# First pair of expert places in strict turns of wide and narrow quarters, with a shorter early load

## The chip, the cores and the metric

The kernel runs on one core of a Trainium2 chip. The metric is the device time of one execution in microseconds, as the median of several runs. TensorE multiplies matrices, VectorE and ScalarE do elementwise work, GpSimd a few powers, and SyncE (SP) issues nearly all DMAs.

## The reference

A hybrid decoder trunk of two layers on 256 tokens of width 1024, float32. Each layer has a mixer (four mLSTM heads beside a diagonal state-space block, joined by an output projection) and a channel mixer. In layer 0 that is a dense SwiGLU of width 2816. In layer 1, which this case is about, it is a routed SwiGLU of eight experts of width 3584, of which each token uses two:

```python
logits = (xt @ w_router).astype(jnp.float32) + b_router.astype(jnp.float32)
top_v, top_i = lax.top_k(logits, TOP_K)
gates = jax.nn.softmax(top_v, axis=-1)
combine = jnp.einsum('tk,tke->te', gates, jax.nn.one_hot(top_i, N_EXPERTS, dtype=jnp.float32))
out = jnp.zeros_like(xt)
for e in range(N_EXPERTS):
    out = out + combine[:, e:e + 1].astype(xt.dtype) * swiglu(xt, w_gate[e], w_up[e], w_down[e])
```

A final RMSNorm follows. The kernel computes an expert only for the tokens that chose it.

## The kernel before

After the router come eight *places*, worked off in pairs (0, 1), (2, 3), (4, 5), (6, 7). Their shapes are fixed by ITEMS = "AEBECDDD" (line 72): A holds 128 tokens, E 32, B 128 + 32, C 64 + 32, D 64. A text below calls the quarters of the first place A0 to A3, those of the second E0 to E3, and the first quarter of the third place B0. Which expert goes to which place is decided on the chip by how many tokens chose it, except that the first place always holds expert 0. Tokens beyond the places' room would be worked off in a loop behind them (MORE, `n_over`), whose length is read from the data.

Each place is cut into four *quarters* of 896 columns of the expert's width. A quarter is: gate and up products (`gate_up`; lines 2279 for 128 tokens, 2293 for 64, 2308 for 32), SiLU on ScalarE and the product on VectorE (`hidden`), the transposes of that (line 2343), and the down products (`down`; lines 2370 and 2381), accumulated in PSUM over the four quarters. The down products of a quarter are issued after the gate and up products of the next one. Between them, at fixed positions of the pair (`between`), stand the gathers of the next place's tokens (line 2256), the transposes of the pick matrix (line 2396) and the scatter of the last pair's result (line 2409). TURNS says in which order the quarters of the two lanes of a pair follow each other: lane 0 is the first place of the pair. FIRST_DONE is the position at which ScalarE copies the first place's finished result out of PSUM.

The weights pass through a ring in SBUF of MSLOT = 18 slots. A gate or up unit (two of eight row blocks, 896 KB) takes one slot and a down unit (1792 KB) two, so a quarter takes 12. `place_units` deals the slots out in the order in which the units were listed, that is in TensorE's order with a quarter's down units behind the gate and up units of the next quarter, and notes for each unit the event that releases the slots it overwrites. A unit of A's gate or up is released when its own matmuls are done, since A has no 32-token part; B's are released only when the whole gate-and-up work of the quarter, with its narrow part (line 2308), is done. SP issues the units in that order and waits before each for its release (`load_unit`, DMA lines 893 and 896). SP has one queue, so a unit that waits holds up all behind it.

The ring lies over the trunk's own weight ring and work space. The *early* units are those with nothing before them in their slots; SP issues them when the trunk's last layer has read the chunks there (`wait_unused`, `hm_ready`), all with expert 0, before it waits on `ranks_ready`, the event that VectorE gives when the list of experts (`n_list`, line 1801) stands. Behind it, SP reads each place's expert number with `value_load` at the first unit of the place.

VectorE writes the list in two parts: `first_tiles` (the order of the experts) right after A's tokens are taken, and `second_tiles` (the overflow) at position 2 of pair 0.

Of the kernel before, what the change touches and what calls it, by code (L numbers as in the profile page):

```python
# [60 lines left out]
MC = 4  # L61
# [11 lines left out]
NI = len(ITEMS)  # L73
# [2 lines left out]
MORE = 6  # L76
COLS = NI + MORE
TMAX = max(CAPS)
TURNS = [(0, 0, 1, 0, 1, 0, 1, 1)] + [(0, 1) * MC] * (NI // 2 - 1)
FIRST_DONE = [len(a) - a[::-1].index(0) for a in TURNS]  # L80


class Experts:


    def __init__(self, last):
# [9 lines left out]
        for p in range(NI // 2):  # L96
            done = [0, 0]
            for pos, lane in enumerate(TURNS[p]):
                self.steps.append((p, pos, 2 * p + lane, done[lane]))
# [368 lines left out]
def trunk_kernel(nc, x, norm_mix, w_in, conv_qk, b_igate, b_fgate, norm_mlstm, s5_a_re, s5_a_im, s5_log_dt,  # L468
# [4 lines left out]
    experts = Experts(banks.last)  # L473
# [4 lines left out]
    with ctx:  # L478
# [236 lines left out]
        def wait_drained(eng, name):  # L715

            _, who, n, _ = banks.at[name]
            eng.wait_ge(drained[who], n)
# [51 lines left out]
        def m_wait_drained(eng, key, k=None):  # L770

            _, who, n, _, _ = experts.at[key]
            eng.wait_ge(m_drained[who], later(n, experts.per_who[who], k))
# [13 lines left out]
        def unit(it, c, kind, h):  # L787

            s, size, _, _ = experts.slot[(it, c, kind, h)]
            return m_ring[:, s:s + size, :].rearrange("p s n -> p (s n)")  # L790
# [23 lines left out]
        def _(sp):  # L814
# [81 lines left out]
                    sp.dma_start(v3(unit(it, c, kind, h), UK),  # L896
                                 src.rearrange("e (k p) n -> p (e k) n", p=P)).then_inc(full, 16)

            early = [u for u in experts.units[:experts.base[3]] if not experts.slot[u[:4]][3]]
            for u in early:  # L900
                s, size, _, _ = experts.slot[u[:4]]
                assert u[0] == 0
# [1582 lines left out]
```

## Time and profile before

| | us |
|---|---|
| median of 3 runs | 1463.04 |
| lowest, highest | 1456.69, 1465.71 |
| the profiled execution, its own time | 1457.26 |
| its span | 1455.1 |
| TensorE matmul busy | 1341.7 (92%) |
| VectorE busy | 470.8 (32%) |
| ScalarE busy | 278.4 (19%) |
| DMA, read | 421.2 MB, 290 GB/s over the span |

The span is the time from the first to the last instruction of the profiled execution. TensorE's busy time is modelled and overlaps its weight loads. The mean granted clock of TensorE was 0.979 of full speed. Times of views are counted from the start of the span. The expert stage begins at 558.8 us, with the first wide matmul of A0, and fills the rest.

### The profile page before, as it was taken

The numbers are of one execution on the slowest core, as the hardware profiler recorded it, in microseconds if no ns is written. First come the engines' busy times: TensorE is split into PE (matmuls) and PEld (weight loads), VectorE is DVE, ScalarE is ACT, GpSimd is POOL, SyncE is SP. The second block draws the span as 40 slices with busy tenths as digits, with TensorE's granted clock in tenths as the row PEclk, the third lists the DMA queues.
The fourth block names the chain that finished last, engine by engine and source line by source line (L and its number), as shares of the span: only waits on it lengthen the run. The fifth ranks groups of instructions, "written<-read, shape, count | busy, mean of one in ns | idle before, by whom it ended". The sixth has DMA issues, their size and how long they took to land.

```text
span 1455.1 us, 18657 instructions
## 1 busy us (share of the span) xinstructions
PE 1341.7 (92%) x7760; PEld 758.9 (52%) x7760; DVE 470.8 (32%) x1049; ACT 278.4 (19%) x515; POOL 98.5 (7%) x115
## 2 busy tenths in 40 slices
PE   6988899999799878999999999999999999987775
PEld 5845489999685535544455444444433344332322
DVE  7995965555589533041010100100110100000002
ACT  2541344443254100000011010001101101000001
POOL 4530000000442000000000000000000000000000
PEclk9999999999999989999999999999999999999999
DMA  9533345436221248799999959889999999999994
GB/s 286 153 116 116 115 164 185 174 116 244 75 87 59 101 191 332 250 363 414 413 411 416 411 213 410 338 353 401 410 411 416 410 410 416 410 412 415 410 414 199
DMA packets 126734, 423.50 MB, mean 291 GB/s; under 512 B 21632, under 2 KB 23864, under 8 KB 118456
## 3 DMA queue, kind: packets, MB, share of 16 engines
q1 hardware_dynamic: 121464, 421.75, 74.2%
q10 hardware_dynamic: 5184, 0.52, 0.4%
q8 instruction: 64, 1.05, 0.3%
q14 instruction: 22, 0.18, 0.0%
HBM read 421.20 MB, written 1.05 MB: 290 GB/s over the span
## 4 chain that ended last, share of the span: by engine, by line
PE 74%; DMA 14%; DVE 8%; issue 1%; SPq 1%; ACT 1%; POOL 0%; DVEq 0%; ACTq 0%
PE psall L2279 13%; DMA m_ring<-in_moe_w_down_dram 12%; PE psall L2370 11%; PE psall L2293 8%; PE psall L2308 6%; PE psall L1992 4%; PE psall L2381 3%; PE psall L2210 3%; PE psall L2090 3%; PE psall L2212 3%; PE psall L2211 3%; PE psall L2157 2%; PE psall L2256 2%; PE psall L2343 2%; PE psall L2409 2%; PE psall L2192 1%
## 5 line engine op out<-in xcount | busy, mean ns | idle before, releaser
L2293 PE MATMUL psall<-m_ring,xeT 128*64 128x448 f32 x1024 | 202.6, 543 | 22.5 <-DMA m_ring<-in_moe_w_up_dram 21.5
L2370 PE MATMUL psall<-m_ring,hidT 128*64 128x512 f32 (+1 forms) x672 | 201.0, 597 | 17.2 <-DMA m_ring<-in_moe_w_down_dram 16.4
L2279 PE MATMUL psall<-m_ring,xeT 128*128 128x448 f32 x512 | 195.7, 543 | 0.8 <-DVE xeT L1857 0.8
L2293 PEld LDWEIGHTS psall<-m_ring,xeT 128*64 128x64 f32 x1024 | 73.6, 137 | 139.9 <-issue 138.8
L2279 PEld LDWEIGHTS psall<-m_ring,xeT 128*128 128x128 f32 x512 | 97.3, 191 | 94.1 <-issue 92.9
L2370 PEld LDWEIGHTS psall<-m_ring,hidT 128*64 128x64 f32 (+1 forms) x672 | 72.6, 154 | 136.3 <-issue 120.1
L1879 DVE TENSOR_TENSOR hid<-e_silu,psall 64x448 f32<-64x448 f32 x32 | 19.9, 623 | 354.6 <-ACT e_silu L1231 352.5
L1577 DVE TENSOR_TENSOR w_lo<-ring,w_hi 128x1024 fp32r<-128x1024 f32 x66 | 80.5, 1225 | 68.0 <-ACT w_hi L1185 67.9
L2308 PE MATMUL psall<-m_ring,xeT 128*32 128x448 f32 x1024 | 102.0, 542 | 0.0
L2210 PE MATMUL psall<-hnT_hi,w_hi 128*128 128x256 f32 x352 | 99.6, 283 | 1.4 <-DVE hnT_lo L1715 1.4
L2212 PE MATMUL psall<-hnT_hi,w_lo 128*128 128x256 f32 x352 | 99.5, 283 | 0.0
L2211 PE MATMUL psall<-hnT_lo,w_hi 128*128 128x256 f32 x352 | 98.9, 281 | 0.0
L1992 PE MATMUL psall<-hnT,ring 128*128 128x256 f32 x384 | 87.1, 386 | 3.0 <-DMA ring<-in_w_in_dram 1.3
L961 POOL TENSOR_TENSOR small<-small,neg_half 128x1 f32<-128x1 f32 (+2 forms) x14 | 13.6, 974 | 1080.1 <-DVE small L1313 970.0
L1875 DVE TENSOR_TENSOR hid<-e_silu,psall 128x448 f32<-128x448 f32 x16 | 9.9, 622 | 227.0 <-PE psall L2279 226.0
L1185 ACT ACTIVATE w_hi<-ring 128x1024 fp32r<-128x1024 f32 x66 | 69.2, 1060 | 63.5 <-PE psall L2212 35.9
L1992 PEld LDWEIGHTS psall<-hnT,ring 128*128 128x128 f32 x384 | 73.3, 193 | 14.5 <-issue 2.1
L1245 ACT ACTIVATE hidT<-psall 128x224 f32<-128x224 f32 (+5 forms) x48 | 22.3, 481 | 266.9 <-PE psall L2343 266.7
L2210 PEld LDWEIGHTS psall<-hnT_hi,w_hi 128*128 128x128 f32 x352 | 66.7, 189 | 2.2 <-issue 1.4
L2211 PEld LDWEIGHTS psall<-hnT_lo,w_hi 128*128 128x128 f32 x352 | 66.6, 189 | 0.8
L2212 PEld LDWEIGHTS psall<-hnT_hi,w_lo 128*128 128x128 f32 x352 | 66.3, 188 | 0.0
L2308 PEld LDWEIGHTS psall<-m_ring,xeT 128*32 128x32 f32 x1024 | 30.4, 109 | 63.6 <-issue 63.0
(326 smaller groups left out, 1473.3 us busy)
## 6 DMA issues: line engine op xcount, KB each, us to landing
m_ring<-in_moe_w_gate_dram SPq DMA_DIRECT2D x128, 896.0 KB, 19.9
m_ring<-in_moe_w_up_dram SPq DMA_DIRECT2D x128, 896.0 KB, 17.1
m_ring<-in_moe_w_down_dram SPq DMA_DIRECT2D x64, 1792.0 KB, 19.1
ring<-in_w_in_dram SPq DMA_DIRECT2D x10, 2048.0 KB, 13.0
ring<-in_ffn_w_gate_dram SPq DMA_DIRECT2D x5, 2048.0 KB, 10.5
ring<-in_ffn_w_up_dram SPq DMA_DIRECT2D x5, 2048.0 KB, 7.7
ring<-in_ffn_w_down_dram SPq DMA_DIRECT2D x5, 2048.0 KB, 8.0
ring<-in_w_out_dram SPq DMA_DIRECT2D x4, 2048.0 KB, 7.9
```

Source lines behind the costliest of these rows:

```text
L1185: nc.scalar.activation(ffn_split(n, w_hi), ffn_raw(n), ACT.Copy).then_inc(ffn_hi, 1)
L1577: V.tensor_tensor(ffn_split(n, w_lo), ffn_raw(n), ffn_split(n, w_hi).bitcast(F32), ALU.subtract).then_inc(ffn_lo, 1)
L1992: ins = M(bank(name)[:, i * SEQ:(i + 1) * SEQ], w[:, k, a:a + P], hnT[:, k, :], start=(k == 0), stop=(k == KT - 1))
L2090: ins = M(bank(n)[:, :], hnT[:, k, n[2] * P:(n[2] + 1) * P], v3(chunk((n[0], l)), KT)[:, k, :], start=(k == 0), stop=(k == KT - 1))
L2210: M(y, hi[:, k, :], hnT_hi[:, k, :], start=(k == 0), stop=False)
L2211: M(y, hi[:, k, :], hnT_lo[:, k, :], start=False, stop=False)
L2212: ins = M(y, lo[:, k, :], hnT_hi[:, k, :], start=False, stop=(k == KT - 1))
L2279: ins = M(m_bank(key)[:, 0:MH], x[:, i, 0:P], weights(kind, i, s), start=(i == 0), stop=(i == KT - 1))
L2293: ins = M(m_bank(key)[64 * n:64 * n + 64, 0:MH], x[:, i, 0:64], weights(kind, i, s), start=(i == 0), stop=(i == KT - 1))
L2308: ins = M(m_bank(key)[q:q + 32, 0:MH], x[:, i, base:base + 32], weights(kind, i, s), start=(i == 0), stop=(i == KT - 1))
L2370: ins = M(y, hidT[:, r, 0:shape[0]], rows(r, 512 * n, 512), **ends)
L2381: ins = M(ps[7][32 * q:32 * q + 32, cols:cols + 256], hidT[:, r, base:base + 32], rows(r, 256 * q, 256), **ends)
```

## The change

The first pair takes the turns that the other pairs have. The early list ends at the first unit of another place than the first, or at the first unit whose slot is taken, whichever comes first.

```diff
-TURNS = [(0, 0, 1, 0, 1, 0, 1, 1)] + [(0, 1) * MC] * (NI // 2 - 1)
+TURNS = [(0, 1) * MC] * (NI // 2)
 FIRST_DONE = [len(a) - a[::-1].index(0) for a in TURNS]
...
-            early = [u for u in experts.units[:experts.base[3]] if not experts.slot[u[:4]][3]]
+            early = []
+            for u in experts.units[:experts.base[3]]:
+                if u[0] or experts.slot[u[:4]][3]:
+                    break
+                early.append(u)
             for u in early:
                 s, size, _, _ = experts.slot[u[:4]]
                 assert u[0] == 0
```

Before, pair 0 runs A0 A1 E0 A2 E1 A3 E2 E3, and the early units are the eight of A0, the eight of A1 and the first down unit of A0. After, it runs A0 E0 A1 E1 A2 E2 A3 E3. The ring's first 18 slots are then listed as A0's eight, E0's eight and A0's first down unit, and only the first eight are early.

## Rows read from the trace of the kernel before

**Rows 1.** The page's DMA issues: tile, queue, count, KB each, us to landing.
```profile
m_ring<-in_moe_w_gate_dram SPq DMA_DIRECT2D x128, 896.0 KB, 19.9
...
m_ring<-in_moe_w_down_dram SPq DMA_DIRECT2D x64, 1792.0 KB, 19.1
```

**Rows 2.** Windows: stretch, us; busy us (instructions) of each engine; clock, DMA share, GB/s.
```profile
640.00:750.00 110.00, 110.00 (x552) 54.82 (x553) 17.86 (x73) 9.13 (x18) 0.00 (x0) 1.00 1.02 413
...
840.00:861.00 21.00, 21.00 (x102) 9.44 (x104) 1.24 (x2) 1.09 (x2) 0.00 (x0) 1.00 0.28 111
...
1300.00:1400.00 100.00, 75.31 (x369) 29.00 (x365) 4.98 (x8) 5.92 (x11) 0.00 (x0) 1.00 1.02 413
```

**Rows 3.** Timeline of SP's queue around the list: start, duration, line, transfer, count.
```profile
533.52 9.26 SPq L896 DMA_DIRECT2D m_ring<-in_moe_w_up_dram  x4
542.83 2.20 SPq L893 DMA_DIRECT2D m_ring<-in_moe_w_down_dram  x1
...
565.13 0.33 SPq L893 DMA_DIRECT2D m_ring<-in_moe_w_down_dram  x1
```

**Rows 4.** Line 896 from 480 to 700 us: issue to landing.
```profile
DMA to landing us min/median/max: 4.7/10.1/22.8
```

**Rows 5.** Windows around the router and A's first two quarters.
```profile
535.00:558.00 23.00, 15.49 (x74) 11.17 (x72) 8.13 (x59) 3.54 (x7) 0.00 (x0) 0.69 1.03 412
565.00:585.00 20.00, 20.00 (x69) 11.08 (x67) 1.24 (x2) 1.09 (x2) 0.00 (x0) 1.00 0.95 327
...
585.00:590.00 5.00, 5.00 (x25) 3.65 (x25) 0.42 (x1) 1.09 (x2) 0.00 (x0) 0.70 0.40 159
```

**Rows 6.** Timeline of VectorE: the cast that writes the expert list.
```profile
562.90 0.17 DVE L1801 CAST n_list<-over 128x8 int32<-128x8 f32 x1
```

**Rows 7.** Timeline of SP's queue where a new place's first unit follows.
```profile
982.79 1.17 SPq L893 DMA_DIRECT2D m_ring<-in_moe_w_down_dram  x2
984.72 0.38 SPq L896 DMA_DIRECT2D m_ring<-in_moe_w_gate_dram  x1
```

**Rows 8.** Timeline of TensorE in pair 0: start, duration, line, operands, count [idle before].
```profile
558.77 24.32 PE L2279 MATMUL psall<-m_ring,xeT 128*128 128x448 f32 x64 [0.78 <-DVE xeT L1857]
582.92 3.65 PE L2256 MATMUL psall<-pick,hn 128*128 128x32 f32 x32
586.41 1.60 PE L2343 MATMUL psall<-ident,hid 128*128 128x128 f32 x7
587.81 25.50 PE L2279 MATMUL psall<-m_ring,xeT 128*128 128x448 f32 x64
613.14 12.18 PE L2370 MATMUL psall<-m_ring,hidT 128*128 128x512 f32 x28
...
626.10 6.22 PE L2308 MATMUL psall<-m_ring,xeT 128*32 128x448 f32 x64
...
644.37 0.60 PE L2396 MATMUL psall<-ident,pickg 128*128 128x128 f32 x4
...
670.12 3.23 PE L2381 MATMUL psall<-m_ring,hidT 128*32 128x256 f32 x56
673.28 1.13 PE L2343 MATMUL psall<-ident,hid 128*128 128x128 f32 x7
...
728.30 3.53 PE L2256 MATMUL psall<-pick,hn 128*128 128x160 f32 x24
...
743.68 1.25 PE L2256 MATMUL psall<-pick,hn 128*128 128x160 f32 x8
...
753.72 3.23 PE L2381 MATMUL psall<-m_ring,hidT 128*32 128x256 f32 x56 [1.66 <-DMA m_ring<-in_moe_w_down_dram]
756.88 1.04 PE L2343 MATMUL psall<-ident,hid 32*128 32x32 f32 x7
757.85 24.32 PE L2279 MATMUL psall<-m_ring,xeT 128*128 128x448 f32 x64
```

**Rows 9.** Window of the list's second part on VectorE (the third busy number).
```profile
634.00:651.00 17.00, 17.00 (x50) 8.51 (x49) 13.96 (x81) 0.95 (x2) 0.00 (x0) 1.00 1.02 417
```

## The prediction, made before the changed kernel was run

> **What bounds the kernel now.** I read the page's DMA issues first: one quarter of an expert is eight units of 896 KB (gate and up) and two of 1792 KB (down), so 12 ring slots of 896 KB, and 32 quarters are 384 slots [rows 1]. Then the stretches. While the expert stage runs freely the DMA share is 1.02 at 413 GB/s, with TensorE busy all the time: 896 KB is 0.9175 MB, so a slot costs 2.22 us and a quarter 26.7 us. At 840 to 861 the share is 0.28: there the stream stands, because the B place's units come free only after its narrow matmuls, and TensorE sets the pace. At 1300 to 1400 the stream is full again and TensorE has idle time; the chain of waits names the transfers there [rows 2]. So the stage has three parts: pair 0 (558.8 to 757.9), near balance; pair 1, led by TensorE; the rest, led by the stream, which restarts from where TensorE's last pair 1 quarter released slots. A shift of the start of B's first quarter (757.9) is therefore handed to the end in full, while a late stream alone has slack in pair 1: about 0.72 x 21 = 15 us at 840 to 861.
>
> **What the old order does with its head start.** SP issues the 17 early units (18 slots) by 545.0 and then has nothing to issue until 565.1, when the first slots of A's quarter 0 come free [rows 3]. The 20 us at 565 to 585 ran at 327 GB/s, and 585 to 590 at a share of 0.40 [rows 5]: with a full ring the stream waits for TensorE. That is where a head start is given back.
>
> **What the change does.** TURNS for pair 0 becomes A0 E0 A1 E1 A2 E2 A3 E3 (A is the wide place, E the narrow one). The unit list follows it, and so does the ring. The early list ends after A0's eight gate and up units; E0's eight and A0's down now wait for the expert list. No instruction of an engine is added or removed, no byte either; FIRST_DONE moves from 6 to 7, so that ScalarE's copy of A's result comes one position later, after the quarter that it needs.
>
> *Taken from the head start:* 10 slots x 2.22 = 22 us of transfers, which before were issued ahead of the list. They can't start before VectorE has cast the list, 562.90 + 0.17 [rows 6]. SP then reads the expert's number; between the last down unit before a new item and its first gate unit the queue shows 983.96 to 984.72, 0.8 us [rows 7]. So the first issue is at 564.0. SP waits there longer than before, but queued behind it are only these same loads; the load of the norm's gains stands ahead of the wait, as before.
>
> *When slots land.* Slots 9 to 18 are free at once. Later ones: slot n needs slot n-18 released. A1's last two (27, 28) need E0's first two, released by 590, with their turn at 606; E1's last two (39, 40) need A1's first two, 613 against 633; A1's down (44) needs A1's sixth unit, 626 against 642; E2's last (64) needs A1's down, 655 against 688. The release is at least 15 us ahead each time. So it runs unbroken at 2.22 us a slot. A unit took 4.7 us to land at the least [rows 4]. Slot n lands at 568.7 + 2.22 (n - 9): E0's last (16) 584.2, A0's down (18, 20) 588.7 and 593.1, E1's last (40) 637.5, A1's down (42, 44) 641.9 and 646.4, E2's last (64) 690.8, A2's down (66, 68) 695.2 and 699.7, E3's last (88) 744.1, A3's down (92) 753.0. In the old order slot 92 (E2's down) released TensorE at 753.7 [rows 8]. So both streams reach the end of pair 0 at the same moment: the old one had 22 us of lead and lost them while the ring was full.
>
> *TensorE's chain, new order* [rows 8]. A's gate and up 24.3, E's 6.15, A's down 12.2, E's down 3.2, A's transposes 1.1 (first time 1.4), E's 1.0, E's gather 3.5, B's 3.4 + 1.2, the pick's transposes 0.5 (these are mostly differences of neighbouring starts, as TensorE's records overlap). From 558.8: A0, gather, transposes 588.0; E0 594.1, A0's down 606.3, transposes 607.3; A1, E0's down, pick, transposes 636.4; E1, A1's down, transposes 655.8 (slots 42 and 44 just in time); A2, E1's down, transposes 684.4. **Now it waits:** E2's last units are wanted at 689.0 and land at 690.8 (1.8), A2's down wanted at 692.3 lands at 695.2 (2.9). Down and transposes end at 708.4; A3, gather, E2's down, transposes 741.7; E3 747.9; A3's down 760.1, transposes 761.1. B's first quarter starts at 761.1 instead of 757.9. The work is the same; waits are 4.7 us instead of 1.7 (752.06 to 753.72). That is +3.2 us.
>
> *Vector and Scalar.* The second part of the list (14 us of VectorE's work at 634 to 651 [rows 9]) now follows A1's product. It ends near 650; E1's product then waits for it and is wanted at 654.8 after A1's down. That down is the cover; without it the part would cost some 6 us. The final copies of A (position 7) lie beside B's 24 us. Both at nothing.
>
> *The clock.* A1's gate and up took 25.50 instead of 24.32, with a granted clock of 0.70 at 585 to 590 [rows 5, 8]: the lower level, 1.2 GHz, for a part of it, behind the short matmuls of gather and transposes. One more such fall is 0 to 1.2 us. In the stretch at 1300 to 1400 TensorE stands idle for short times many times over and the clock is 1.00 [rows 2]. I take 0.8, between the ends, since the two new waits are longer than those. [...]
>
> **Sum:** 3.2 + 0.8 = +4 us. Unknown costs: stream rate and landing -1.7 (no wait left at all, chain without the old 1.7) to +8 (slots landing 4 to 5 us later than the formula). Against the profiled execution: 1457.3 + 4 = 1461.3 (span 1455.1 + 4). That execution is 5.8 us under the median shown, 1463.0, and the runs spread from 1456.7 to 1465.7; in the median's terms 1467. I name 1466.5, a little toward the profile.
>
> **Rivals.**
> *R1, the head start is paid in full.* Place: E0 and after. If all that follows is led by the stream, 10 slots later is 22 us later: 1485. For it: the stream is full from 640 to 750 [rows 2]. Against it: in the old order it idles at 585 to 590 with a full ring [rows 5], and TensorE leads pair 1. It decides, beyond 1%, once slot 68 lands after 711 instead of 699.7, which is a mean of 380 GB/s over 60 slots; units fed one by one ran at 327 [rows 5], and 60 slots at that rate would take 168 us, 35 more than at 413. So it needs a stream that starves for slots. The Trainium skill (DMA: Bandwidth & Descriptors, Rules for kernel authors) says to issue a DMA early, compute, and wait for it late; taken alone it speaks against this change, and by it the price is those 22 us. Chance 0.12 (half of it in full, the rest 10 to 20 us).
> *R2, no wait is left.* The old order's own waits go, the stream lands 5 us earlier than my formula, and TensorE runs through pair 0: 558.8 + 197.4 = 756.2, -1.7 us: 1461. For it: the formula's landing time is one for a lone unit, and the waits are small. Against it: slot 92 of the old order lands within 1 us of the formula's time for the new one. It turns on whether slots 64 and 66 land by 689.0 and 690.6. Chance 0.12.
> *R3, faster.* The router's stretch gains from a quiet DMA: at 535 to 558 the share is 1.03 and the clock 0.69 [rows 5]. Yet TensorE waits there for VectorE's short steps, not for transfers. At most a few us, and over 1% only if something outside this account moves. Chance 0.04.
> *Forecast* (+2 to +8, no change that can be told): 0.72.
>
> **Numbers.** About 1% (14.6 us) is what a measurement of this kernel can tell from no change. Forecast and R2 lie inside it; of R1 some 0.10 lies beyond, of R3 0.03. Faster 0.03, same 0.87, slower 0.10. The range adds to the forecast's bounds (1461 to 1471 in the median's terms) the spread of the medians that the runs allow, some 4 us below and 6 above: 1457 to 1477; it leaves out R1 nearly whole, and R3's far end.
>
> **What would show it.** In the profile after: first E0 load at about 564 and a DMA share near 1.0 from 566 to 750; E0's narrow matmuls at 588 without a wait; waits of 2 to 5 us for transfers around 690 to 700; B's first wide matmul at 760 to 764; from there each line of TensorE shifted by the same 3 to 6 us, and a span near 1459. It is wrong if pair 0 shows holes in the stream (R1), if B starts at or before 757 (R2), or if pair 1 gives the shift back, which would mean that TensorE didn't lead it.

## The result, and the profile after

The changed kernel takes 1463.48 us (median of 20 runs, 1459.78 to 1467.82) against 1458.60 us for the kernel before in the same comparison. The ratio is 1.0031, 95% interval 1.0019 to 1.0042: 4.5 us, between 2.8 and 6.1 (the two medians differ by 4.9), so slower by less than a measurement of three runs could tell. The median of three runs shown ahead, 1463.04, was at the high end of the kernel before; 20 runs put it 4.4 us lower. The profiled execution has a span of 1458.9 us, 3.8 more than before.

Windows of the changed kernel: stretch, us; busy us of each engine; clock, DMA share, GB/s.

```profile
565.00:585.00 20.00, 20.00 (x67) 10.95 (x65) 1.24 (x2) 1.09 (x2) 0.00 (x0) 1.00 1.01 391
585.00:590.00 5.00, 5.00 (x36) 3.29 (x39) 0.42 (x1) 1.09 (x2) 0.00 (x0) 0.72 1.01 427
640.00:750.00 110.00, 106.17 (x532) 51.74 (x524) 17.29 (x71) 7.24 (x15) 0.00 (x0) 0.98 1.02 413
690.00:700.00 10.00, 6.50 (x31) 2.10 (x24) 1.24 (x2) 1.07 (x2) 0.00 (x0) 0.83 1.01 425
840.00:861.00 21.00, 21.00 (x69) 10.15 (x71) 1.24 (x2) 1.09 (x2) 0.00 (x0) 1.00 0.47 185
1300.00:1400.00 100.00, 76.63 (x378) 29.65 (x374) 3.74 (x6) 6.29 (x12) 0.00 (x0) 1.00 1.02 413
```

Read them against [rows 2, 5]. At 565 to 585 the stream moves 391 GB/s instead of 327, and at 585 to 590 it is full where it stood at a share of 0.40. It doesn't run out of free slots any more, because it starts behind. Its rate when full is the same 413 GB/s. TensorE now has 3.8 us of idle time at 640 to 750, where it had none. In pair 1 (840 to 861) there is still a hole, a smaller one: 0.47 instead of 0.28.

SP's queue around the expert list, and VectorE's cast that writes the list:

```profile
526.97 4.33 SPq L896 DMA_DIRECT2D m_ring<-in_moe_w_up_dram  x4
531.71 0.35 SPq L914 DMA_DIRECT2D bT<-in_norm_final_dram  x1
564.29 0.40 SPq L896 DMA_DIRECT2D m_ring<-in_moe_w_gate_dram  x1
...
570.59 3.00 SPq L893 DMA_DIRECT2D m_ring<-in_moe_w_down_dram  x2
```

```profile
563.14 0.17 DVE L1805 CAST n_list<-over 128x8 int32<-128x8 f32 x1
```

The queue is silent from 532.1 to 564.3. The first load stands 0.98 us behind the cast's end. All ten remaining slots of the first round are issued by 573.6.

TensorE in pair 0 and at the start of pair 1, down to E3's down products (the last row): start, duration, line, operands, count, [idle time before, what ended it].

```profile
559.01 24.32 PE L2283 MATMUL psall<-m_ring,xeT 128*128 128x448 f32 x64 [0.78 <-DVE xeT L1861]
...
588.19 7.42 PE L2312 MATMUL psall<-m_ring,xeT 128*32 128x448 f32 x64
...
608.72 24.32 PE L2283 MATMUL psall<-m_ring,xeT 128*128 128x448 f32 x64
...
638.04 6.22 PE L2312 MATMUL psall<-m_ring,xeT 128*32 128x448 f32 x64
...
657.38 24.32 PE L2283 MATMUL psall<-m_ring,xeT 128*128 128x448 f32 x64
...
685.85 4.72 PE L2312 MATMUL psall<-m_ring,xeT 128*32 128x448 f32 x48
692.94 3.16 PE L2312 MATMUL psall<-m_ring,xeT 128*32 128x448 f32 x16 [2.37 <-DMA m_ring<-in_moe_w_up_dram]
697.23 12.26 PE L2374 MATMUL psall<-m_ring,hidT 128*128 128x512 f32 x28 [1.13 <-DMA m_ring<-in_moe_w_down_dram]
...
743.56 6.22 PE L2312 MATMUL psall<-m_ring,xeT 128*32 128x448 f32 x64
750.52 12.25 PE L2374 MATMUL psall<-m_ring,hidT 128*128 128x512 f32 x28 [0.74 <-DMA m_ring<-in_moe_w_down_dram]
...
763.68 24.32 PE L2283 MATMUL psall<-m_ring,xeT 128*128 128x448 f32 x64
...
797.77 3.23 PE L2385 MATMUL psall<-m_ring,hidT 128*32 128x256 f32 x56
```

Three waits for transfers, at E2's last units, at A2's down and at A3's down, make 4.24 us; before there was one of 1.66 [rows 8]. E0's narrow matmuls took 7.42 us instead of 6.22 at a granted clock of 0.72 (585 to 590), which stands for the 1.2 us that A1 lost in the same place before. And the last 16 matmuls of E2, behind the 2.37 us wait, took 3.16 us; 16 of the same kind behind a 1.08 us wait in a run below took 1.71. B0 begins 204.7 us behind A0 instead of 199.1. The chain of waits between 670 and 780 goes through the last two of the three transfers:

```profile
678.35 18.75 DMA m_ring<-in_moe_w_down_dram
...
697.23 12.26 PE psall L2374 x28
...
730.82 19.56 DMA m_ring<-in_moe_w_down_dram
...
750.52 12.25 PE psall L2374 x28
```

So A2's down starts when slot 66 lands, A3's down when slot 90 lands, and what TensorE lost ahead of them only shortened its waits.

The chain that ended last names the same transfer as before, a down unit at the end of the last pair, 3.8 us later: it is followed from 1413.84 (before 1409.99) to TensorE's last down products at 1440.66 (before 1436.82).

```profile
1413.84 26.77 DMA m_ring<-in_moe_w_down_dram
1440.62 0.04 issue
1440.66 3.68 PE psall L2374 x16
```

### The profile page after: what moved, and what is told of

The parts are those of the page before. It is cut to its first block, busy times and chain, and to the rows that moved or that the text cites. A ratio compares the mean times of both kernels' runs of the same rounds, so it can differ in the third digit from the quotient of the medians.

```text
span 1458.9 us, 18655 instructions
## 1 busy us (share of the span) xinstructions
PE 1343.2 (92%) x7760; PEld 757.4 (52%) x7760; DVE 470.5 (32%) x1049; ACT 278.1 (19%) x515; POOL 98.0 (7%) x115
## 4 chain that ended last, share of the span: by engine, by line
PE 73%; DMA 15%; DVE 8%; issue 1%; ACT 1%; SPq 1%; POOL 0%; DVEq 0%; ACTq 0%
DMA m_ring<-in_moe_w_down_dram 13%; PE psall L2283 13%; PE psall L2374 12%; PE psall L2297 8%; PE psall L2312 5%; PE psall L1996 4%; PE psall L2214 3%; PE psall L2216 3%; PE psall L2094 3%; PE psall L2215 3%; PE psall L2385 3%; PE psall L2161 2%; PE psall L2260 2%; PE psall L2413 2%; PE psall L2347 2%; PE psall L2196 1%
## 5 line engine op out<-in xcount | busy, mean ns | idle before, releaser
L2374 PE MATMUL psall<-m_ring,hidT 128*64 128x512 f32 (+1 forms) x672 | 201.2, 597 | 19.4 <-DMA m_ring<-in_moe_w_down_dram 18.6
```

Source lines behind the costliest of these rows:

```text
L2374: ins = M(y, hidT[:, r, 0:shape[0]], rows(r, 512 * n, 512), **ends)
```

## The experiments

Theory 1: the change costs what the stream of weights lacks at E2 and at A's downs, because 10 slots are loaded behind the list instead of ahead of it; the strict turns cost nothing themselves. Theory 2: the turns cost it. R1: the lost head start is paid in full. Edits are shown against the changed kernel; those of old_late, old_pair1 and old_pair12 are made to the kernel before.

The beginning of A0 differs between profiled executions by up to 10 us, though nothing ahead of it differs but the loads. So the stage is compared from A0's start (computed from the timelines; the last column is the start of TensorE's last down products, which the last transfer releases).

| kernel | A0 | B0 - A0 | C0 - A0 | last down - A0 | ratio to before (95%) |
|---|---|---|---|---|---|
| before | 558.8 | 199.1 | 454.9 | 878.1 | |
| changed | 559.0 | 204.7 | 458.6 | 881.7 | 1.0031 (1.0019 to 1.0042) |
| strict_head17 | 559.6 | 198.7 | 454.5 | 877.8 | 1.0004 (0.9992 to 1.0017) |
| old_cut8 | 566.5 | 199.3 | 455.3 | 878.4 | 1.0000 (0.9988 to 1.0013) |
| strict_early9 | 556.8 | 200.5 | 454.7 | 878.0 | 1.0006 (0.9990 to 1.0022) |
| strict_late | 563.7 | 218.9 | 475.0 | 898.2 | 1.0125 (1.0105 to 1.0145) |
| old_late | 559.1 | 199.1 | 455.0 | 878.3 | 1.0006 (0.9989 to 1.0022) |
| old_pair1 | 564.7 | 199.4 | 454.6 | 868.4 | 0.9931 (0.9907 to 0.9955) |
| strict_pair1 | 559.4 | 204.9 | 459.5 | 873.2 | 0.9964 (0.9948 to 0.9979) |
| old_pair12 | 561.9 | 201.2 | 456.6 | 867.5 | 0.9906 (0.9887 to 0.9924) |

### strict_head17: the new turns with the whole head start

```diff
-                if u[0] or experts.slot[u[:4]][3]:
+                if experts.slot[u[:4]][3]:
                     break
...
-                load_unit(u, slice(0, 1))
+                load_unit(u, slice(u[0], u[0] + 1))
```

> Strict turns in pair 0 as in the changed kernel, but all 17 units with free slots are issued ahead of the list again: E0's gate and up are loaded with expert 1's weights instead of those that the list names, so this part of the result is another. Theory 1 (the late transfers cost it): slots 9 to 18 are there by 560, no wait near 690, B0 starts at 757 to 759, ratio to the kernel before 0.999 to 1.001, some 4 us under the changed kernel. Theory 2 (the order of the turns costs it, through later copies and narrower cover): B0 stays near 763, ratio 1.003.

This kernel leaves out the look-up of the expert for E0's gate and up and takes expert 1's, so its result is another, with the same bytes and the same matmuls.

Measured: 1.0004. TensorE of this kernel around 690:

```profile
686.41 6.22 PE L2311 MATMUL psall<-m_ring,xeT 128*32 128x448 f32 x64
692.56 12.28 PE L2373 MATMUL psall<-m_ring,hidT 128*128 128x512 f32 x28
...
758.26 24.32 PE L2282 MATMUL psall<-m_ring,xeT 128*128 128x448 f32 x64
```

E2 and A2's down follow each other without a wait and at full speed, and B0 comes 198.7 us after A0, 0.4 earlier than in the old order. The old order's 199.1 us contain a wait of 1.66 for a transfer and these 198.7 none, so TensorE's own chain is 1.3 us longer in the new turns, and the wait that they avoid pays for it. On balance the turns cost nothing that can be measured; Theory 2 falls.

### old_cut8: the old turns with only eight units ahead

```diff
-TURNS = [(0, 1) * MC] * (NI // 2)
+TURNS = [(0, 0, 1, 0, 1, 0, 1, 1)] + [(0, 1) * MC] * (NI // 2 - 1)
...
-                if u[0] or experts.slot[u[:4]][3]:
+                if len(early) == 8:
                     break
```

> The old turns, with only A0's eight units ahead of the list: A1's eight and A0's first down unit wait for it. Theory 1: slot n lands at 568.7 + 2.22 (n - 9); A1's last unit lands at 584 and is wanted behind 588, slot 92 lands at 753.0 against 753.7 before, so the cut of the head start alone costs +0.5 us (0 to +2.5), ratio 1.000 to 1.002. Rival R1 (the head start is paid in full): +22 us, 1.015. Theory 2: 1.000, as it blames the turns.

Measured: 1.0000. The same 22 us of transfers are moved behind the list, and nothing is lost. SP's queue, then TensorE:

```profile
570.84 2.32 SPq L896 DMA_DIRECT2D m_ring<-in_moe_w_gate_dram  x4
573.20 3.72 SPq L896 DMA_DIRECT2D m_ring<-in_moe_w_up_dram  x4
576.96 2.97 SPq L893 DMA_DIRECT2D m_ring<-in_moe_w_down_dram  x2
```

```profile
566.51 24.32 PE L2283 MATMUL psall<-m_ring,xeT 128*128 128x448 f32 x64 [0.78 <-DVE xeT L1861]
595.54 25.60 PE L2283 MATMUL psall<-m_ring,xeT 128*128 128x448 f32 x64
...
761.64 3.23 PE L2385 MATMUL psall<-m_ring,hidT 128*32 128x256 f32 x56 [1.75 <-DMA m_ring<-in_moe_w_down_dram]
```

The one wait is the old one, at E2's down: 1.75 us instead of 1.66. R1 falls: in this order the head start beyond eight units buys nothing. So neither half of the change costs anything alone that can be measured; the cost is that of both together. In the kernel before, slots 64 and 66 are A3's last unit and E1's down, wanted at 715 and 718 (A3 starts at 693.68 and reaches its last unit 21 us on):

```profile
693.68 24.32 PE L2279 MATMUL psall<-m_ring,xeT 128*128 128x448 f32 x64
717.93 3.23 PE L2381 MATMUL psall<-m_ring,hidT 128*32 128x256 f32 x56
...
792.05 4.75 PE L2381 MATMUL psall<-m_ring,hidT 128*32 128x256 f32 x56
```

In the strict turns they are E2's last unit and A2's down, wanted some 25 us sooner, at about 690 and 693, while a stream that starts at the list brings them at 693 and 697. (The last row, E3's down in the kernel before, is used further down.)

### strict_early9: one more unit ahead

```diff
-                if u[0] or experts.slot[u[:4]][3]:
-                    break
-                early.append(u)
+                if u[0] == 0 and not experts.slot[u[:4]][3]:
+                    early.append(u)
...
-            for u in experts.units[len(early):experts.base[3]]:
+            for u in [u for u in experts.units[:experts.base[3]] if u not in early]:
```

> Strict turns, and A0's first down unit (2 slots, expert 0, known ahead) is issued ahead of the list beside A0's eight, out of its place in the queue. Theory 1: every slot from 19 on lands 4.4 us earlier than in the changed kernel; the waits there of 2.37, 1.13 and 0.74 us shrink to under 1 in all, and the fall of the clock behind the first goes with them (1.6 us). Ratio to the kernel before 1.000 to 1.001, B0 at 758 to 760. Theory 2: ratio 1.003, B0 near 763.

Measured: 1.0006. Two slots, 4.4 us of transfers, take back 4.1 us at B0:

```profile
683.59 6.22 PE L2311 MATMUL psall<-m_ring,xeT 128*32 128x448 f32 x64
690.89 12.26 PE L2373 MATMUL psall<-m_ring,hidT 128*128 128x512 f32 x28 [1.08 <-DMA m_ring<-in_moe_w_down_dram]
...
744.15 12.26 PE L2373 MATMUL psall<-m_ring,hidT 128*128 128x512 f32 x28 [0.71 <-DMA m_ring<-in_moe_w_down_dram]
```

The 2.37 us wait is gone, and with it the slow matmuls behind it; the waits at the two downs stay, 1.79 us in all where I had expected under 1. This kernel has the changed one's turns and computes the same, without a cost that can be measured (its B0 still comes 1.5 us later than before, its C0 no longer).

### strict_late and old_late: the same late list in both orders

```diff
             sp.wait_ge(ranks_ready, 1)
+            sp.wait_ge(m_ready, experts.free[("uh", 0, 0, 1)])
```

> The changed kernel, but SP waits for the list and also for A0's sixth unit to be used (near 577 instead of 564). Theory 1: pair 0 is led by the stream from E0 on, all slots land 13 us later, and nothing gives it back: B0 near 776, +13 us over the changed kernel, ratio to the kernel before 1.011 to 1.013. If the stream had slack in pair 0 (R2's view, waits only by chance) the shift would be under 8 us, ratio under 1.009.

> The kernel before, but SP waits for the list and also for A0's sixth unit to be used (near 577 instead of 565), as strict_late does with the strict turns. Theory 1: 18 slots are already there, TensorE needs slot 20 at 618 and E0's at 626, and the stream's idle time between 585 and 625 takes up the 13 us: 0 to +2 us, ratio 1.000 to 1.001. So the same delay costs 13 us in the one order and head start and nothing in the other. If a late list costs the same in both, the ratio is 1.009.

Measured: 1.0125 and 1.0006. With the strict turns SP's first load comes 19.35 us behind A0's start instead of 5.28, so 14.1 later, and B0 comes 14.2 us later:

```profile
583.07 0.40 SPq L896 DMA_DIRECT2D m_ring<-in_moe_w_gate_dram  x1
```

```profile
599.60 1.71 PE L2313 MATMUL psall<-m_ring,xeT 128*32 128x448 f32 x16 [2.21 <-DMA m_ring<-in_moe_w_up_dram]
604.08 1.71 PE L2313 MATMUL psall<-m_ring,xeT 128*32 128x448 f32 x16 [2.77 <-DMA m_ring<-in_moe_w_up_dram]
608.38 13.95 PE L2375 MATMUL psall<-m_ring,hidT 128*128 128x512 f32 x28 [2.59 <-DMA m_ring<-in_moe_w_down_dram]
...
658.35 1.71 PE L2313 MATMUL psall<-m_ring,xeT 128*32 128x448 f32 x16 [1.08 <-DMA m_ring<-in_moe_w_up_dram]
```

E0 already waits, which it does not in the changed kernel. Over the runs the delay costs 0.0094, 13.7 us, as expected; this one execution ends 16.5 us later than the changed one, and of the 2.3 us above B0's shift, which it loses in pair 1, 1.7 are a slow narrow quarter right behind E3's down (7.92 us, in the changed kernel 6.22); the rest is not explained. With the old turns and 17 units the same wait costs nothing, and the old wait at E2's down is 1.70 us. SP's first load behind the list, then TensorE:

```profile
577.44 0.33 SPq L893 DMA_DIRECT2D m_ring<-in_moe_w_down_dram  x1
```

```profile
754.06 3.23 PE L2382 MATMUL psall<-m_ring,hidT 128*32 128x256 f32 x56 [1.70 <-DMA m_ring<-in_moe_w_down_dram]
...
758.19 24.32 PE L2280 MATMUL psall<-m_ring,xeT 128*128 128x448 f32 x64
```

So the changed kernel's pair 0 is tied to the moment at which the list stands, microsecond for microsecond over this delay, and that of the kernel before is not. These two runs differ in head start as well as in order, so they don't say which of the two ties it; old_cut8, with eight units ahead and the old turns, loses nothing by a stream that starts at the list, so it isn't the head start alone.

### old_pair1, strict_pair1 and old_pair12: who sets the end

```diff
-TURNS = [(0, 0, 1, 0, 1, 0, 1, 1)] + [(0, 1) * MC] * (NI // 2 - 1)
+TURNS = [(0, 0, 1, 0, 1, 0, 1, 1), (0, 1, 1, 0, 1, 0, 0, 1)] + [(0, 1) * MC] * (NI // 2 - 2)
```

(strict_pair1: the same second entry in the changed kernel. old_pair12: also (0, 1, 1, 0, 0, 0, 1, 1) for pair 2.)

> The kernel before with pair 1 (B = 128 + 32 tokens, and E) in the turns B E E B E B B E instead of strict ones. Theory 1 says that the end is set by the stream, which restarts when pair 1's last wide quarter releases its slots at 982 in one burst; with two wide quarters next to each other before the last narrow one, the last burst comes some 20 us earlier in TensorE's order, so the stream is further ahead at pair 2: C's first quarter starts at the same time (1011 to 1016) but the end is 8 to 12 us earlier, ratio 0.992 to 0.995. Rival: TensorE alone leads up to C0 and what follows is merely added to it: ratio 1.000.

> The changed kernel with the same turns of pair 1 (B E E B E B B E). If pair 0's shift is handed on through pair 1 whatever its order, this is the changed kernel's +4.5 us on top of old_pair1's gain: ratio 0.995 to 0.998. If the new pair 1 gives slack to the stream, the two kernels with it are equal (0.992 to 0.995).

> old_pair1 with pair 2 (C = 64 + 32 tokens, and D) in the turns C D D C C C D D as well. By the same account, 1 to 2 us better than old_pair1: ratio 0.991 to 0.994. If the stream is full without a gap from 1020 on, pair 2's turns can give nothing: equal to old_pair1.

Measured: 0.9931, 0.9964 and 0.9906. C0 begins where it did (454.6 us behind A0, before 454.9), but the last down comes 9.7 us sooner. Windows of old_pair1:

```profile
840.00:861.00 21.00, 21.00 (x142) 10.82 (x135) 1.23 (x2) 3.11 (x6) 0.00 (x0) 1.00 1.03 414
...
1060.00:1100.00 40.00, 40.00 (x249) 13.34 (x249) 5.26 (x8) 2.69 (x5) 0.00 (x0) 1.00 1.00 385
```

and of old_pair12:

```profile
1060.00:1100.00 40.00, 40.00 (x229) 15.26 (x233) 4.01 (x6) 2.76 (x5) 0.00 (x0) 1.00 1.02 415
```

The hole at 840 to 861 [rows 2] is closed. TensorE's last wide quarter of pair 1 releases its slots at 974.8, 410.1 us behind A0, instead of 422.8 (before: 975.39 + 6.22 = 981.6). In old_pair1:

```profile
944.32 24.32 PE L2279 MATMUL psall<-m_ring,xeT 128*128 128x448 f32 x64
968.57 6.22 PE L2308 MATMUL psall<-m_ring,xeT 128*32 128x448 f32 x64
```

C0 comes at the same distance and the end sooner, so the end is set by the stream and not by TensorE's arrival at pair 2. That it hangs on the moment of that release is worked out: the release comes 12.7 us sooner, the hole at 1060 to 1100 that is told of below takes back 2.9, which leaves 9.8, and 9.7 were measured. The closed hole at 840 to 861 alone would not do it, since another is deeper than before: the stream moves 221 GB/s at 961 to 981, against 324 in the kernel before.

strict_pair1 ends 4.9 us behind old_pair1, counted from A0 (3.1 by the medians, 1452.91 against 1449.81), so pair 0's loss is handed through either order of pair 1. old_pair12 closes a small hole at 1060 to 1100 (385 to 415 GB/s, 1.2 MB or 2.9 us) and has the lowest time of all, 1444.76 us; its interval overlaps that of old_pair1, so the step from one to the other is likely and not shown. Counted from A0 its last down comes only 0.9 us sooner: in this execution C0 came 2.1 us later behind A0 than in old_pair1, with E2's down slow in pair 0 (4.92 us instead of 3.23, behind a wait of 2.07). Both beat both kernels of this study.

## Why the prediction was right

The forecast was +4 us, no change that can be told; measured +4.5. Step by step:

- *The stream's start, 564.0*: 564.29. Right, as was "without a gap": the share is 1.01 to 1.02 up to 750.
- *Slots land at 568.7 + 2.22 (n - 9)*: slot 64 released TensorE at 692.9 instead of 690.8, slot 66 at 697.1 instead of 695.2, slot 90 at 750.4 instead of 748.5. The rate is right, and the constant is 2 us short: I took the landing time of the quickest single unit. From 564.0 to 697.09 the DMA moved 407 GB/s, 54.2 MB, and the 58 slots from 9 to 66 hold 53.2. The difference, by estimate 2 us of the stream, are parts of units behind slot 66 that came before its last bytes; a lone unit's time doesn't contain them. (A slip without effect: slot 64 overwrites A2's second unit, free at about 664, and not A1's down.)
- *TensorE's waits, 4.7 us*: 4.24 us, but otherwise placed. E2's last units 2.37 (predicted 1.8), A2's down 1.13 (2.9), A3's down 0.74 (none, although my own formula has slot 90 at 748.5 and my chain wants it at 747.9).
- *The clock, 0.8*: the falls came, and at B0 this term was nothing. E2's last 16 matmuls ran at half speed behind the 2.37 us wait and lost 1.5 us; A2's down would have waited for those 1.5 us anyway, so its own wait was shorter by as much. What I had left out of the chain is the slow stretch at 585 to 590, 1.2 us, which the old order's chain contained. It moved from A1 to E0, and the waits behind it took it up too. Without waits it counts: strict_head17 took 198.7 us to B0, where my chain at full speed has 197.4.
- *B0 at 761.1*: 763.7, 5.8 us later than before (5.6 counted from A0) and not 3.2. A2's down began at 697.2 instead of 695.2, and A3's down waited 0.7 us: these two, both from the landing times, are the difference.
- *From B0 on each line shifted alike*: wrong in size. At C0 the shift is 3.95, because E3's down (797.77) took 3.23 us and not 4.75 as in the kernel before, a fall of the clock that this execution does not have, and by small amounts later. strict_head17 has the slow one, strict_early9 has not, and in strict_late and strict_pair1 the narrow quarter behind it is slow instead (7.92 us for 6.22). The sum put +4.0 at B0, which came at +5.6 to 5.8, and the missing fall gave 1.6 back. So it was right within 0.5 us partly by luck: the landing times were 2 us too early, and a gain that was not forecast made up for it.
- *The list's second part and the final copies, at nothing*: right. Behind A1's down the transposes of E1 follow at 656.41 without a wait.
- *R1, its price*: old_cut8 measured its price, 22 us expected and 0 found. The Trainium skill asks to issue transfers early, since the fixed setup cost then overlaps (DMA: Bandwidth & Descriptors, Rules for kernel authors); the 22 us were my price and not the page's. This case agrees with the rule only as far as the lead is used: in the old order 10 slots of lead are worth nothing, in the strict one the first two are worth nearly all of the 4.5 us (1.0006 against 1.0031).
- *The late list*: the prediction said that pair 0 was led by the stream in the new order, and strict_late shows it with its 14.2 us for 14.1.
- *Pair 1 led by TensorE, a shift handed on in full*: right that it is handed on (strict_pair1), but the account of the end was only half told. A shift of TensorE's arrival at pair 2 and a shift of the last burst of releases in pair 1 came together here; old_pair1 moved the second without the first, and the end went with the second.

## What to carry to other kernels

A lead in a ring of buffers is worth only what the consumer can use before the ring is full again: find the first place where the consumer outruns the stream, count the slots up to it, and compare the landing time with the time at which it is wanted. Order and head start have to be judged together, since here neither alone cost anything that could be measured. And where the stream sets the end, look for the last moment at which it had to stop for a burst of releases, even far ahead: reordering the consumer there gained 10 us, more than twice what the first pair's turns and loads had cost.

## What the runs showed that I had not expected

A single wait of 2.37 us behind narrow matmuls was followed by matmuls at half speed (3.16 us for 16, at a granted clock of 0.83 over 690 to 700), while in strict_late waits of 2.21 and 2.77 us in a row, among the same matmuls, were followed by full speed (1.71 us for 16), and only the down behind the third, 2.59 us, was slow (13.95 us instead of 12.25). In the same kernel two more downs followed a wait of 2.58 us each, one at 662.65 slow (13.95) and one at 716.14 at full speed (12.25). Which wait brings a fall isn't settled by its length alone. A like fall comes and goes at E3's down (4.75 or 3.23 us for 56 matmuls, 4.92 in strict_head17) without any wait there. And the trunk ahead of the stage, which no kernel changes, ended anywhere from 556.8 to 566.5 us: more than what was to be measured, so that only many runs, or times counted from A0, could show 4.5 us.
